# Scattering weighted expert rows by an accumulating DMA into one row per token

## The chip, the cores and the metric

The kernel runs on one core of a Trainium2 chip. The metric is the device time of one execution in microseconds (us). A profiled execution gives the trace; its own span and time stand in the table below.

## The reference, cut to what matters

```python
h = x + hybrid_mixer(rms_norm(x, norm_mix_g), ...)          # 512 tokens x 1024
xf = rms_norm(h, norm_ffn_g)
logits = xf @ w_router + b_router                            # 32 experts
top_vals, top_idx = lax.top_k(logits, 4); top_w = softmax(top_vals)
for each expert e, over the tokens that chose it:
    gu = x_e @ w_gate_up[e] + b_gate_up[e]                   # 1024 -> 2048
    gate = min(gu[:, :1024], 7); up = clip(gu[:, 1024:], -7, 7)
    y = ((up + 1) * gate * sigmoid(1.702 * gate)) @ w_down[e] + b_down[e]
    out[token] += top_w * y                                  # four experts for each token
return rms_norm(h + out, norm_final_g)
```

All numbers are float32. Each token has four choices, so there are 2048 (token, choice) pairs.

## The kernel before, in words

The first 670 us are the mixer, the router and the routing tables. The change bears on the second part, `mix_and_experts`, which each engine has once, and there on the experts.

**Items.** An item is one expert with up to 128 slots, one slot in each partition. Item i reads the weights of expert i; a second round of items exists only where an expert has more than 128 tokens. `last` is the number of the last item, here 31. `target` holds for each slot and item the number 4 x token + choice, or a number from 2048 up for an empty slot; `index` is `target` shifted right by two, which is the token.

**The loop.** Each engine runs a hardware loop over i = 0 to last - 1, and what is left of item `last` stands behind it.
- SyncE (SP) loads 12 chunks of 1 MB of weights per item into the six slots of `mraw`, each as soon as the chunk six before it is split.
- ScalarE rounds a chunk to float32r (`mhi`, L512), VectorE subtracts to get the rest (`mlo`, L516), TensorE takes three products of each pair: L2330, L2331 and L2333 for gate and up of item i + 1, L2351, L2352 and L2354 for down of item i.
- After the first chunk of down, TensorE turns the tokens `xg` that were gathered for item i + 2 (`turn_tokens`, L2308). It waits there for the gather.
- ScalarE copies the finished rows of item i from PSUM to `y_rows` (`y_copy`, L1280).
- GpSimd (POOL) does per pass: the product `hid` (L888); `scatter(i)`, a copy of a column of `target` to `now` (L891), a wait for `y_copy`, a tiny addition (`step`, L876), an indirect DMA of `y_rows` to memory (L895) and a wait until it has landed; then `gather(i + 3)`, a copy of a column of `index` (L879), `step`, and an indirect DMA that brings the tokens (L882).

The scatter writes row `target` of `y_d`, 2048 rows of 4 KB, one for each (token, choice) pair; empty slots are out of bounds and are left out. The rows of the last item are not scattered.

**The end.** When the last scatter has landed, POOL releases SP (`s_stored`). SP loads `norm_final_g` (L727) and then, for each of the four tiles of 128 tokens, the four rows of each of its tokens, 2 MB in two DMAs (L737). VectorE adds three of the four rows with their weights to the residual `h_rows` (`add_rows`, L1867). TensorE gathers in PSUM the down biases (`bias_product`, L2392), the rows of the last item through the 0/weight matrix `put_back` (`last_rows`, L2398) and the fourth row of each token through a diagonal of weights (`fourth_rows`, L2404). VectorE adds that (`add_products`, L1875), ScalarE sums squares (L1324), POOL makes the inverse root (L947, L949), VectorE scales (`finish`, L1880) and SP stores the tile (L741).

The order around the change is set by hand, by the program order of each engine and its semaphores:

```python
def scatter(i):
    nc.gpsimd.tensor_copy(now[:, 1:2], target[:, bass.ds(i, 1)]).then_inc(s_goal, 1)
    pool.wait_ge(s_goal, i + 1)
    pool.wait_ge(s_y, i + 2)
    step()
    nc.gpsimd.indirect_dma_start(y_d, ... now[:, 1:2] ..., y_rows[:], ...).then_inc(s_yst, 16)
    pool.wait_ge(s_yst, 16 * i + 16)
    pool.sem_inc(s_yfree, 1)
```

Names as the profile writes them: `zT` is `h_rows`, `glu` holds gate, up, sig and hid, `qkvT` holds `xn2`, `PB` is PSUM, `expert_rows_scratch` is `y_d`, `xn_scratch` holds the normed tokens.

## Time and profile before

| | us |
|---|---|
| median of 3 runs | 1855.16 (1854.9 to 1856.78) |
| the profiled execution's own time | 1855.72 |
| its span | 1854.0 |
| TensorE busy | 1805.2 (97%) |
| VectorE busy | 1473.2 (79%) |
| ScalarE busy | 1103.4 (60%) |
| GpSimd busy | 411.1 (22%) |

Granted TensorE clock over the span: 0.993 of full speed. The 16 DMA engines moved 507.80 MB, 274 GB/s on the mean. A busy TensorE is one whose matmuls follow each other; the time between the profiled execution and its span lies outside the span.

### The profile page before, as it was taken

How to read it: one execution, taken by the hardware profiler on the slowest of the kernel's cores; microseconds unless marked ns; L12 is line 12 of the kernel's file. 1: busy time of each engine (PE TensorE's matmuls, PEld its weight loads, DVE VectorE, ACT ScalarE, POOL GpSimd, SP SyncE). 2: the span in 40 equal slices, each digit the busy share in tenths (PEclk: the TensorE clock that was granted, in tenths of full speed). 3: DMA queues.
4: the chain of work that ended last, by engine and by line, in shares of the span. 5: the costliest groups of instructions: out<-in, count | busy, mean ns of one | idle time of the engine just before them, and what ended most of it. 6: DMA issues, size and time to landing. Idle time of an engine off the chain costs nothing.

```text
span 1854.0 us, 23922 instructions
## 1 busy us (share of the span) xinstructions
PE 1805.2 (97%) x8636; PEld 1502.9 (81%) x8636; DVE 1473.2 (79%) x1101; ACT 1103.4 (60%) x906; POOL 411.1 (22%) x332
## 2 busy tenths in 40 slices
PE   7999999999999999999999999999999999999995
PEld 6888888798888887888888888888888888888873
DVE  4236666765334689999999999999999999999996
ACT  4223563333332346777777777777777777777771
POOL 0000112420000018222222321322322222232231
PEclk9999999999999999999999999999999999999998
DMA  5323423005572538999999999999999999999976
GB/s 165 111 91 110 163 87 119 18 7 178 197 243 98 227 137 329 364 382 382 350 382 380 352 371 385 356 370 382 357 366 382 379 346 380 382 347 380 381 282 239
DMA packets 129774, 507.80 MB, mean 274 GB/s; under 512 B 26327, under 2 KB 26535, under 8 KB 95620
## 3 DMA queue, kind: packets, MB, share of 16 engines
q1 hardware_dynamic: 118276, 490.69, 69.4%
q0 software_dynamic: 9280, 16.27, 2.3%
q8 instruction: 29, 0.48, 0.1%
q10 hardware_dynamic: 2176, 0.26, 0.1%
q14 instruction: 13, 0.11, 0.0%
HBM read 492.46 MB, written 32.02 MB: 283 GB/s over the span
## 4 chain that ended last, share of the span: by engine, by line
PE 89%; DVE 6%; ACT 2%; DMA 1%; issue 1%; SPq 0%; POOL 0%; DVEq 0%; POOLq 0%; ACTq 0%
PE PB L2330 12%; PE PB L2331 12%; PE PB L2333 12%; PE PB L2249 11%; PE PB L2354 6%; PE PB L2351 6%; PE PB L2352 6%; PE PB L1934 4%; PE PB L1936 4%; PE PB L1935 4%; PE PB L2067 2%; PE PB L2320 2%; PE PB L2314 1%; PE PB L2308 1%; PE PB L2214 1%
## 5 line engine op out<-in xcount | busy, mean ns | idle before, releaser
L516 DVE TENSOR_TENSOR mlo<-mraw,mhi 128x2048 fp32r<-128x2048 f32 x384 | 906.5, 2395 | 48.2 <-ACT mhi L512 46.7
L512 ACT ACTIVATE mhi<-mraw 128x2048 fp32r<-128x2048 f32 x384 | 721.5, 1913 | 110.0 <-PE PB L2333 110.0
L2330 PE MATMUL PB<-mhi,xgT_hi 128*128 128x512 f32 x1024 | 403.1, 394 | 1.3 <-DVE mlo L516 1.3
L2331 PE MATMUL PB<-mlo,xgT_hi 128*128 128x512 f32 x1024 | 400.0, 391 | 0.0
L2333 PE MATMUL PB<-mhi,xgT_lo 128*128 128x512 f32 x1024 | 273.9, 389 | 0.0
L2330 PEld LDWEIGHTS PB<-mhi,xgT_hi 128*128 128x128 f32 x1024 | 192.7, 188 | 42.3 <-DVE mlo L516 1.4
L2333 PEld LDWEIGHTS PB<-mhi,xgT_lo 128*128 128x128 f32 x1024 | 192.3, 188 | 40.3
L2331 PEld LDWEIGHTS PB<-mlo,xgT_hi 128*128 128x128 f32 x1024 | 192.9, 188 | 39.5
L2351 PE MATMUL PB<-mhi,hT_hi 128*128 128x512 f32 x512 | 202.1, 395 | 1.1 <-DVE hT_lo L1831 1.1
L2352 PE MATMUL PB<-mlo,hT_hi 128*128 128x512 f32 x512 | 199.4, 389 | 0.0
L888 POOL TENSOR_TENSOR glu<-glu 128x1024 f32<-128x1024 f32 x32 | 78.8, 2462 | 522.5 <-DVE glu L1826 522.5
L2354 PE MATMUL PB<-mhi,hT_lo 128*128 128x512 f32 x512 | 158.0, 390 | 0.0
L1367 DVE TENSOR_TENSOR lo<-raw,hi 128x2048 fp32r<-128x2048 f32 x24 | 55.0, 2291 | 114.8 <-ACT hi L979 114.8
L1934 PE MATMUL PB<-xT_hi,hi 128*128 128x512 f32 x336 | 131.2, 390 | 0.7 <-ACT ab L1001 0.7
L1679 DVE TENSOR_TENSOR lo<-qkvT,hi 128x2048 fp32r<-128x2048 f32 x18 | 41.3, 2292 | 113.2 <-ACT hi L1192 113.2
L1935 PE MATMUL PB<-xT_lo,hi 128*128 128x512 f32 x336 | 130.7, 389 | 0.0
L1936 PE MATMUL PB<-xT_hi,lo 128*128 128x512 f32 x336 | 130.7, 389 | 0.0
L979 ACT ACTIVATE hi<-raw 128x2048 fp32r<-128x2048 f32 x26 | 49.8, 1914 | 127.8 <-PE PB L1936 105.0
L2351 PEld LDWEIGHTS PB<-mhi,hT_hi 128*128 128x128 f32 x512 | 96.2, 188 | 20.3 <-issue 1.5
L2354 PEld LDWEIGHTS PB<-mhi,hT_lo 128*128 128x128 f32 x512 | 96.1, 188 | 20.1
L2352 PEld LDWEIGHTS PB<-mlo,hT_hi 128*128 128x128 f32 x512 | 96.3, 188 | 18.9
L1192 ACT ACTIVATE hi<-qkvT 128x2048 fp32r<-128x2048 f32 x18 | 34.5, 1915 | 120.0 <-PE PB L2249 115.6
(359 smaller groups left out, 2572.9 us busy)
## 6 DMA issues: line engine op xcount, KB each, us to landing
mraw<-in_w_gate_up_dram SPq DMA_DIRECT2D x256, 1024.0 KB, 7.3
mraw<-in_w_down_dram SPq DMA_DIRECT2D x128, 1024.0 KB, 8.8
raw<-in_w_in_dram SPq DMA_DIRECT2D x28, 1024.0 KB, 5.1
qkvT<-in_w_in_dram SPq DMA_DIRECT2D x8, 1024.0 KB, 5.1
expert_rows_scratch<-zeros SPq DMA_DIRECT2D x4, 2048.0 KB, 11.4
mraw<-expert_rows_scratch SPq DMA_DIRECT2D x6, 1024.0 KB, 11.8
qkvT<-in_w_o_gdn_dram SPq DMA_DIRECT2D x4, 1024.0 KB, 6.4
qkvT<-in_w_o_sconv_dram SPq DMA_DIRECT2D x4, 1024.0 KB, 5.1
```

The costliest lines, as they stand in the source:

```text
L512: nc.scalar.activation(mhi[split_slot(m)][:], mraw[:, raw_slot(m), :], ACT.Copy).then_inc(e_h, 1)
L516: nc.vector.tensor_tensor(mlo[split_slot(m)][:], mraw[:, raw_slot(m), :], mhi[split_slot(m)][:].bitcast(F32), ALU.subtract).then_inc(e_l, 1)
L1934: pe.matmul(dst, w_hi, xT_hi[:, k, :], start=(k == 0), stop=False)
L1935: pe.matmul(dst, w_hi, xT_lo[:, k, :], start=False, stop=False)
L1936: mm = pe.matmul(dst, w_lo, xT_hi[:, k, :], start=False, stop=(k == KD - 1))
L2249: mm = pe.matmul(dst, lhsT, rhs, start=(k == 0 and n == 0), stop=(k == KD - 1 and n == 2))
L2330: pe.matmul(gate_up_bank[:, n, :], xgT_hi[:, k, :], w_hi[:, n, :], start=False, stop=False)
L2331: pe.matmul(gate_up_bank[:, n, :], xgT_hi[:, k, :], w_lo[:, n, :], start=False, stop=False)
L2333: mm = pe.matmul(gate_up_bank[:, n, :], xgT_lo[:, k, :], w_hi[:, n, :], start=False, stop=(k == KD - 1))
L2351: pe.matmul(y_bank[:, n, :], hT_hi[:, k, :], w_hi[:, kk, n, :], start=(k == 0), stop=False)
L2352: pe.matmul(y_bank[:, n, :], hT_hi[:, k, :], w_lo[:, kk, n, :], start=False, stop=False)
L2354: mm = pe.matmul(y_bank[:, n, :], hT_lo[:, k, :], w_hi[:, kk, n, :], start=False, stop=(k == KD - 1))
```

## The change

The scratch `y_d` of 2048 rows is replaced by `sum_d` of 512 + 128 rows, one row for each token and 128 spare ones. SP stores the residual `h_rows` to the first 512 (four DMAs of 512 KB, ahead of the loop) and clears the spare ones (one DMA of 512 KB; before, four DMAs of 2 MB cleared `y_d`). `scatter` adds in memory: its DMA has `compute_op=ALU.add`, takes the row from `index`, and an empty slot of partition p goes to spare row 512 + p (the table of targets is numbered so), so that all 128 rows are moved each time. The weights are applied before the scatter: `y_copy` multiplies each partition by `slot_weight`, a column that an indirect DMA (`slot_weights`) brings for the next item right behind each scatter, by a second copy into `now[:, 2:3]`. `put_back` is 0/1 and `by_weight` is gone. At the end SP loads one row per token (512 KB for each tile), straight into `h_rows`; the added rows (`add_rows`) and the fourth rows (`fourth_rows`) are gone.

```diff
-    y_d = nc.dram_tensor("expert_rows_scratch", (SEQ * TOPK, D), F32, kind="Internal").ap()
+    sum_d = nc.dram_tensor("token_sums_scratch", (SEQ + P, D), F32, kind="Internal").ap()
...
@@ SP
-                        if 2 <= g <= TT + 1:
+                        if g == 2:
                             sp.wait_ge(s_zeros, 1)
-                            sp.dma_start(y_d.rearrange("(t p r c) d -> t p (r c d)", t=TT, p=P, r=1)[g - 2].rearrange(
-                                "p (n c) -> p n c", c=GW), zeros[:].unsqueeze(1).to_broadcast([P, TOPK * D // GW, GW])
-                                         ).then_inc(s_ycl, 16)
+                            sp.dma_start(sum_d[SEQ:].rearrange("p (n c) -> p n c", c=GW),
+                                         zeros[:].unsqueeze(1).to_broadcast([P, D // GW, GW])).then_inc(s_ycl, 16)
...
                         sp.dma_start(xn2_d.rearrange("(t p) d -> p t d", p=P)[:, t, :], xn2[:, t, :]).then_inc(s_store, 16)
+                    for t in range(TT):
+                        sp.dma_start(sums_by_token[:, t, :], h_rows[:, t, :]).then_inc(s_hout, 16)
...
                     sp.wait_ge(s_stored, 1)
                     sp.dma_start(final_gain[:], norm_final_g.partition_broadcast(P)).then_inc(s_fg, 16)
                     for t in range(TT):
-                        if t == 0:
-                            sp.wait_ge(e_l, chunk_number(last, 0))
-                        elif t < TT - 1:
-                            sp.wait_ge(e_l, chunk_number(last, 2 * t - 1) + 1)
-                        else:
-                            sp.wait_ge(e_used, chunk_number(last, 3) + 1 + SPL)
-                        for half in range(2):
-                            w = slice(half * 2 * D, (half + 1) * 2 * D)
-                            sp.dma_start(rows_t[t].rearrange("p k d -> p (k d)")[:, w], y_by_token[t][:, w]
-                                         ).then_inc(s_pick[t][half], 16)
+                        sp.dma_start(h_rows[:, t, :], sums_by_token[:, t, :]).then_inc(s_back[t], 16)
@@ POOL
                     def scatter(i):
-                        nc.gpsimd.tensor_copy(now[:, 1:2], target[:, bass.ds(i, 1)]).then_inc(s_goal, 1)
+                        nc.gpsimd.tensor_copy(now[:, 1:2], index[:, bass.ds(i, 1)]).then_inc(s_goal, 1)
+                        pool.wait_ge(s_ws, 16 * i + 16)
+                        nc.gpsimd.tensor_copy(now[:, 2:3], target[:, bass.ds(i + 1, 1)]).then_inc(s_wrow, 1)
                         pool.wait_ge(s_goal, i + 1)
+                        pool.wait_ge(s_wrow, i + 2)
                         pool.wait_ge(s_y, i + 2)
                         step()
-                        nc.gpsimd.indirect_dma_start(y_d, bass.IndirectOffsetOnAxis(ap=now[:, 1:2], axis=0), y_rows[:], None,
-                                                     bounds_check=SEQ * TOPK - 1, oob_is_err=False).then_inc(s_yst, 16)
+                        nc.gpsimd.indirect_dma_start(sum_d, bass.IndirectOffsetOnAxis(ap=now[:, 1:2], axis=0), y_rows[:], None,
+                                                     compute_op=ALU.add, bounds_check=SEQ + P - 1, oob_is_err=True
+                                                     ).then_inc(s_yst, 16)
+                        slot_weights()
                         pool.wait_ge(s_yst, 16 * i + 16)
                         pool.sem_inc(s_yfree, 1)
+
+                    def slot_weights():
+                        nc.gpsimd.indirect_dma_start(slot_weight, None, w_d, bass.IndirectOffsetOnAxis(ap=now[:, 2:3], axis=0),
+                                                     bounds_check=SEQ * TOPK - 1, oob_is_err=False).then_inc(s_ws, 16)
...
-                    for t in range(TT):
-                        n = t * TOPK + TOPK - 1
-                        nc.gpsimd.tensor_scalar(by_weight[:, t, :], ident[:], weight[:, n:n + 1], None, ALU.mult).then_inc(s_byw, 1)
...
+                    pool.wait_ge(s_hout, 16 * TT)
@@ ACT
                         act.wait_ge(s_yfree, i + 1)
-                        nc.scalar.activation(y_rows[:].rearrange("p (b c) -> p b c", b=2), y_bank, ACT.Copy).then_inc(s_y, 1)
+                        act.wait_ge(s_ws, 16 * i + 16)
+                        nc.scalar.activation(y_rows[:].rearrange("p (b c) -> p b c", b=2), y_bank, ACT.Copy,
+                                             scale=slot_weight).then_inc(s_y, 1)
@@ DVE
                     def add_products(t):
+                        dve.wait_ge(s_back[t], 16)
                         dve.wait_ge(s_bo, 2 * t + 2)
-                        dve.wait_ge(s_added, added[0])
...
-                    add_rows(0, range(3))
-                    for t in range(TT):
-                        if t + 1 < TT:
-                            add_rows(t + 1, range(2))
+                    for t in range(2):
                         add_products(t)
-                        if t + 1 < TT:
-                            add_rows(t + 1, range(2, 3))
+                    dve.wait_ge(s_sum, 1)
+                    finish(0)
+                    for t in range(2, TT):
+                        add_products(t)
+                    dve.wait_ge(s_sum, TT)
+                    for t in range(1, TT):
                         finish(t)
@@ PE
                     last_rows(0)
-                    fourth_rows(0)
                     last_rows(1)
                     last_rows(2)
                     bias_product(3)
                     last_rows(3)
-                    for t in range(1, TT):
-                        fourth_rows(t)
```

One pass of POOL's loop before, from `hid` to the gather (ISA and REGISTER_ALU set registers):

```order
L888 TENSOR_TENSOR glu<-glu 128x1024
L891 ISA
L891 COPY now<-target 128x1
L876 TENSOR_TENSOR idle<-idle 128x1
L895 DMA expert_rows_scratch<-y_rows,now 2048x1024
L897 ISA
L879 ISA
L879 COPY now<-index 128x1
L876 TENSOR_TENSOR idle<-idle 128x1
L882 DMA xg<-xn_scratch,now 128x1024
```

and the same piece of POOL's loop with the change, where the lines of the changed file are counted:

```order
L877 TENSOR_TENSOR glu<-glu 128x1024
L880 ISA
L880 COPY now<-index 128x1
L881 ISA
L882 ISA
L882 COPY now<-target 128x1
L865 TENSOR_TENSOR idle<-idle 128x1
L887 DMA token_sums_scratch<-y_rows,now 640x1024
L895 DMA goal_f<-choice_weights_scratch,now 128x1
```

A second one-column copy stands between the first and the step, and a second indirect DMA behind the scatter; the copy of `index`, the step and the gather follow as before.

VectorE behind its loop, before (`zT` is `h_rows`; the first two rows of these are the last weight splits):

```order
L516 TENSOR_TENSOR mlo_88<-mraw,mhi_84 128x2048
L1867 SCALAR_TENSOR_TENSOR zT<-mraw,weight,zT 128x1024 x5
L1875 TENSOR_TENSOR zT<-PB,zT 128x1024
L1867 SCALAR_TENSOR_TENSOR zT<-mraw,weight,zT 128x1024
L1880 SCALAR_TENSOR_TENSOR zT<-zT,fstat,final_gain 128x1024
L1867 SCALAR_TENSOR_TENSOR zT<-mraw,weight,zT 128x1024 x2
L1875 TENSOR_TENSOR zT<-PB,zT 128x1024
```

and VectorE's whole end with the change:

```order
L515 TENSOR_TENSOR mlo_88<-mraw,mhi_84 128x2048
L1862 TENSOR_TENSOR zT<-PB,zT 128x1024 x2
L1867 SCALAR_TENSOR_TENSOR zT<-zT,fstat,final_gain 128x1024
L1862 TENSOR_TENSOR zT<-PB,zT 128x1024 x2
L1867 SCALAR_TENSOR_TENSOR zT<-zT,fstat,final_gain 128x1024 x3
```

All twelve additions of weighted rows are gone, and three of the four scalings stand at the very end.

## Rows read from the trace of the kernel before

**Rows 1.** One item's length: busy us of PE, PEld, DVE, ACT, POOL; clock; DMA share; GB/s.

```profile
1400.00:1435.40 35.40, 35.40 (x166) 29.42 (x165) 33.81 (x18) 26.54 (x18) 9.40 (x7) 1.00 0.95 371
```

**Rows 2.** Waits of PE from 745 us to the end: total, times, longest us.

```profile
PE PB L2404 <- DMA rows<-expert_rows_scratch: 3.0, 1, 3.0
```

**Rows 3.** Timeline of POOL through item 30: start us, us, what, idle before.

```profile
1762.85 2.39 POOL L888 TENSOR_TENSOR glu<-glu 128x1024 f32<-128x1024 f32 x1 [17.22 <-DVE glu L1826]
1765.20 2.24 POOL L891 COPY now<-target 128x1 uint32 x1
1768.59 1.06 POOL L876 TENSOR_TENSOR idle<-idle 128x1 f32<-128x1 f32 x1 [1.15 <-ACT y_rows L1280]
1769.81 1.07 POOL L895 DMA_INDIRECT expert_rows_scratch<-y_rows,now  x1 [0.15 <-issue]
1778.46 0.76 POOL L879 COPY now<-index 128x1 uint32 x1 [7.58 <-DMA expert_rows_scratch<-y_rows,now]
1779.31 0.19 POOL L876 TENSOR_TENSOR idle<-idle 128x1 f32<-128x1 f32 x1
1780.00 1.06 POOL L882 DMA_INDIRECT xg<-xn_scratch,now  x1 [0.50 <-issue]
```

**Rows 4.** Timeline of VectorE in the same stretch.

```profile
1763.81 5.79 DVE L516 TENSOR_TENSOR mlo<-mraw,mhi 128x2048 fp32r<-128x2048 f32 x2
1770.28 8.90 DVE L516 TENSOR_TENSOR mlo<-mraw,mhi 128x2048 fp32r<-128x2048 f32 x4 [0.68 <-ACT mhi L512]
1779.10 1.22 DVE L1831 TENSOR_TENSOR hT_lo<-PB,hT_hi 128x1024 fp32r<-128x1024 f32 x1
1780.30 6.83 DVE L516 TENSOR_TENSOR mlo<-mraw,mhi 128x2048 fp32r<-128x2048 f32 x3
```

**Rows 5.** Timeline of PE's weight loads: the turn of the gathered tokens.

```profile
1793.35 1.02 PEld L2308 LDWEIGHTS PB<-ident,xg 128*128 128x128 f32 x8
```

**Rows 6.** From issue to landing, the scatter L895, then the gather L882.

```profile
DMA to landing us min/median/max: 3.3/7.6/9.0
...
DMA to landing us min/median/max: 5.3/8.0/8.4
```

**Rows 7.** Columns as rows 1: the last scatter's data, then a stretch of the closing loads.

```profile
1806.80:1808.30 1.50, 1.50 (x7) 1.24 (x8) 1.23 (x1) 1.50 (x2) 0.00 (x0) 1.00 0.42 159
1823.00:1825.00 2.00, 2.00 (x6) 0.91 (x5) 1.90 (x2) 0.00 (x0) 0.00 (x0) 1.00 0.99 414
```

**Rows 8.** Columns as rows 1: the stretch behind the stores of `xn2`.

```profile
660.00:672.00 12.00, 12.00 (x109) 12.00 (x109) 8.28 (x28) 3.51 (x3) 0.95 (x1) 1.00 0.12 46
```

**Rows 9.** POOL ahead of its loop's first `hid`, then at the last scatter.

```profile
735.86 2.41 POOL L888 TENSOR_TENSOR glu<-glu 128x1024 f32<-128x1024 f32 x1 [3.72 <-DVE glu L1826]
...
1805.23 1.07 POOL L895 DMA_INDIRECT expert_rows_scratch<-y_rows,now  x1 [0.16 <-issue]
```

**Rows 10.** The end: the chain that ended last, one wait of it.

```profile
1811.54 10.80 DMA mraw<-expert_rows_scratch
```

**Rows 11.** The end: timeline of PE.

```profile
1818.59 1.96 PE L2398 MATMUL PB<-y_rows,put_back 128*128 128x512 f32 x4 [0.31 <-ACT y_rows L1319]
1820.38 1.88 PE L2404 MATMUL PB<-mraw,by_weight 128*128 128x512 f32 x4
1825.13 1.03 PE L2392 MATMUL PB<-b_out,mix_wT 96*128 96x512 f32 x2
```

**Rows 12.** The end: timeline of VectorE, and SP's load L727 with its landing.

```profile
1825.15 1.23 DVE L1875 TENSOR_TENSOR zT<-PB,zT 128x1024 f32<-128x1024 f32 x1
1828.59 1.28 DVE L1880 SCALAR_TENSOR_TENSOR zT<-zT,fstat,final_gain 128x1024 f32<-128x1024 f32 x1 [1.02 <-POOL fstat L949]
...
1848.29 1.28 DVE L1880 SCALAR_TENSOR_TENSOR zT<-zT,fstat,final_gain 128x1024 f32<-128x1024 f32 x1 [2.15 <-POOL fstat L949]
...
1810.14 0.34 SPq L727 DMA_DIRECT2D final_gain<-in_norm_final_g_dram  x1
...
DMA to landing us min/median/max: 4.4/4.4/4.4
```

More of the change, by code:

```diff
@@ L2398, in last_rows @@
                             pe.matmul(PM[:, BANK_OF_TILE[t] + n, :], put_back[:, t * P:(t + 1) * P],
[L2399 to L2405 removed]
+                                      y_rows[:, n * GW:(n + 1) * GW], start=False, stop=True).then_inc(s_bo, 1)
                     pe.wait_ge(s_mixc, 1)
```

59 lines of the change are left out of this document (20 added, 39 removed).

## The prediction

> **What bounds the kernel now.** First the busy time of one stretch as long as an item, from the middle of the loop [rows 1]: TensorE is busy in all of its 35.40 us, VectorE in 33.81, and the DMA engines are at 0.95 with 371 GB/s. Then the waits of TensorE from 745 us on [rows 2]: in 31 passes of the loop it waits for nobody worth a row, and its longest wait, 3.0 us, is at the end, for the last rows that come back. So the loop is worth something only if the change makes TensorE wait, and a gain has to come from the end. There the chain has one wait of 10.80 us for a load of expert rows [rows 10]; the eight loads of 1 MB keep the engines at 0.99 and 414 GB/s [rows 7], VectorE adds rows between them, and its last scaling starts at 1848.29 [rows 12], though TensorE had the last item's rows at 1818.59 [rows 11].
>
> A second thing is to be read before the sum: how POOL's small operations go. A one-element step takes 0.19 us at 1779.31, while VectorE reads PSUM (L1831, 1779.10 to 1780.31), and 1.06 us at 1768.59; the copy of one column takes 2.24 us at 1765.20 [rows 3]. The 1.06 ends at 1769.65, with the second of the two subtractions L516 that began at 1763.81 and ran 5.79 us in all, to 1769.60; the next begins 0.68 us later [rows 3, 4]. So a small POOL operation begun under L516 ends with it. The next four end by 1779.18, then come L1831 and three more, of 6.83 us: ends at about 1782.6, 1784.9 and 1787.1 [rows 4].
>
> **The loop, step by step**, with item 30's times. Before, the scatter is issued at 1769.81, seen landed and followed by the copy at 1778.46 (8.65 later), the gather is issued at 1780.00 [rows 3], lands 8.0 later (median) [rows 6], 1788.0, and TensorE takes the tokens at 1793.35 [rows 5]. Slack: 5.3 us.
> - *Second copy.* It starts at 1767.5, under L516, and ends at 1769.65. `y_copy` was awaited until 1768.59, so 1.1 us of it lies in a wait that was there. The step then starts at about 1769.9 and fits into the gap up to 1770.28 [rows 4]. Scatter at about 1770.25: +0.4 us. Bounds: 0, and +2.8 if the step misses the gap (it then ends with the next L516, at 1772.6). I take 0.4, since the gap of 0.68 us holds a 0.19 us step and two waits.
> - *The scatter itself.* Before there is no accumulating DMA, so its price has to be bounded. The last scatter, alone on the engines, is the cleanest row: its data moved in 1.50 us at a share of 0.42 and 159 GB/s, 0.24 MB or 58 rows [rows 7]. Now 128 rows go, and each is also read from memory. From below, nothing: less than half of the engines' time was used, so 70 more rows could fit beside the 58, with the reading hidden. From above, all in proportion: 128/58 rows times two passes is 4.4 times 1.50, 6.6 us, +5.1. I take +1.5, a doubling of the data phase: the unused share holds the new rows and the second read is paid. The row it is nearest to is the 1.50.
> - The Trainium skill, Collectives: The Full Stack, "The bandwidth ceiling: the fold count and why AG ≠ RS ≠ AR", says that an adding DMA is slower not by the add but by its two source reads, which halve its rate. By that too the data phase doubles; without it (the add free and the read hidden) the term would be 0 and the sum about 1 us lower. No run here shows it yet.
> - *`slot_weights`.* A DMA_INDIRECT costs POOL 1.07 us [rows 3], here inside the 7.58 us wait for the scatter: nothing. If that cover were gone it would be 1.1 us on the way to the gather. What queues behind it is only `gather(i + 3)`. `y_copy` needs its column one item later, some 25 us after it lands: nothing.
> - *`y_copy` with a per-row scale.* Nothing: up to 1.06 us more (1769.65 less 1768.59) hides behind the second copy.
> - *The gather behind it.* Copy of `index` ready at 1770.25 + 8.65 + 1.5 = 1780.4. That is just under the first of the three L516, so copy until 1782.65, then the step under the second until 1784.9, gather at about 1785.1, landed 8.0 later at 1793.1. TensorE asks at 1793.35. Slack 0.25 us; at the longest landing seen, 8.4 [rows 6], 0.15 us late. A scatter at its median of 7.6 instead of item 30's longer one has its copy ready near 1779.6, beside L1831, and the gather leaves 4 us earlier. So most items wait for nothing; I allow 1 us over the loop.
> - *The queue of weights.* Per item the scatter writes 0.26 MB more (64 rows more, since 2048 pairs over 32 items are 64 per item) and reads 0.52 MB: 0.79 MB in 35.4 us, 22 GB/s on 371. The closing loads show 414 [rows 7], so 393 fits: nothing.
>
> **The start.** Four stores of 0.5 MB more on SP, ahead of the loop: 2.1 MB are 5.1 us at 414 GB/s, and the engines are at 0.12 from 660 to 672 [rows 8], where they fall: nothing. If that cover were gone, the first weights would come 5 us later. The 7.9 MB of clears less lie under mixer products with TensorE busy: nothing. Without `by_weight` POOL is earlier at its first `hid`, where it waited 3.72 us for VectorE already [rows 9]: nothing.
>
> **The end.** The last scatter left at 1805.23 [rows 9]; now the second copy holds it until about 1805.65. It landed after 3.3 us [rows 6]; with +1.5 it lands at 1810.5. The copy of `index` then falls under the last L516 (to 1811.6), and SP is released some 0.7 us after it, at about 1812.3, where its load of the gain stood at 1810.14 [rows 12]: +2.2. Behind it come 2.1 MB instead of 8.4. The gain took 4.4 us alone [rows 12]; 0.5 MB are 1.3 us at 414 GB/s, so the tiles land at about 1818, 1819.3, 1820.6 and 1822. TensorE is later than that: a tile of `last_rows` takes 1.79 us (1818.59 to 1820.38) and the bias product about 0.9 of the 1.03 shown [rows 11], so tiles end at 1820.5, 1822.2, 1824.0 and 1826.4. The loads have left the path. Even with +5.1 for the scatter the first tile comes at 1821.6 and the last at 1825.6, which costs nothing at the last tile.
>
> VectorE: additions of 1.23 us [rows 12] at 1820.6 and 1822.3; the first scaling 2.2 us after the end of its addition, as before (1825.15 + 1.23 to 1828.59 [rows 12]), so 1824.1 to 1825.3; additions to 1826.5 and 1827.7; scalings of tiles 1 and 2 to 1829.0 and 1830.2. The last could start 2.25 us after 1827.7, at 1830.0, and starts at 1830.2. Before, it started at 1848.29: **-18.1 us**. The store behind it is the same, though three now follow each other closely.
>
> **Sum.** -18.1 + 1 + 0 = -17.1 on the profiled execution's own 1855.72 gives 1838.6; the median of the runs is 0.56 lower, so **1838 us**. Measurements of this kernel tell about 0.2% (3.7 us) from no change; below, faster and slower mean by more than that.
>
> **The rivals.**
> - *TensorE starves for tokens (slower).* If the copy of `index` is ready after 1782.6 instead of 1780.4, it ends with the second L516 (1784.9), the step with the third (1787.1), the gather leaves at 1787.3 and lands at 1795.3, 2.0 us after TensorE asks. Every later engine shifts with TensorE, so it is paid in each pass: 30 x 2.0 = 60 us, 1838 + 60 = 1898. It decides at a scatter 3.7 us dearer than item 30's before, or 1.2 us dearer with a missed gap. For it: the bound of +5.1, and slack already used up by two quanta. Against it: the engines' unused 0.58 in rows 7. Chance 0.20, of which a part falls on some items only.
> - *Small waits in the loop.* The slack of 0.25 us is overdrawn by 0.15 to 0.5 us in most items, by a longer landing under a fuller queue: 5 to 15 us, 1842 to 1853. Chance 0.13.
> - *The memory is full already.* The loop is at 0.95; if 393 GB/s is more than loads mixed with stores can reach (the 414 are loads alone) and the ceiling is, say, the 371 shown, then each item takes 0.79 MB / 371 GB/s = 2.1 us longer, 31 x 2.1 = 66, 1904. Against it: 0.05 of the engines' time is free, and 414 in the same kernel. Chance 0.03.
> - The Trainium skill, HBM Reference, "Specifications (TRN2)", gives 358 GB/s as a core's share of the memory, and that a core alone gets about 425. By the share the loop would be over the limit already and the change could only cost (0.79 MB are 2.2 us then, 1906); the rows with 371 and 414 agree with the figure for a core alone.
> - *The end does not pay.* The tiles come back late or TensorE's part is longer than worked out, so only half of the 18 is won: 1846 or so. Chance 0.04.
>
> **The numbers.** Forecast, 1834 to 1842: 0.60. Small waits 0.13, half an end 0.04, starving 0.20, full memory 0.03. Faster: 0.60 + 0.11 + 0.04 + a little of the partly starved = 0.76; same 0.04; slower 0.20. Below 1833 lies next to nothing (the end would have to gain over 22). Up to 1866 lie the forecast, the small waits and the cases where fewer than half the items starve: 0.80.
>
> **What would show it.** Right: the item's length stays 35.4 us with TensorE busy throughout; POOL's second copy of about 2.2 us; scatter to landing about 9.5 us in the loop and 4.8 at the last; the gather issued 1 to 5 us later in the item; no additions L1867 at the end, tiles landed before TensorE's products, the last scaling some 18 us earlier. Wrong: a wait of TensorE at the turn of `xg` for the gather, 31 times; an item longer than 35.4; scatter to landing above 12 us; ScalarE waiting for weights.

## The result, and the profile after

The changed kernel takes **1872.93 us** (median of 4 runs, 1871.05 to 1875.78); the kernel before, beside it on the same chip, 1855.97 us (4 runs, 1854.90 to 1857.27). The ratio is 1.0092, 95% interval 1.0077 to 1.0107: slower by 17 us, where 17 us less were forecast. 1872.93 lies 7 us above the upper end of the range. One slow execution of the kernel before, of 3723 us, beside the first experiments is left out of all ratios.

The first and the last `hid` of POOL cut the span into three parts. In the profiled executions (spans 1854.0 and 1871.4, clock 0.995 after the change) they give:

| part | before, us | after, us | difference | forecast |
|---|---|---|---|---|
| start to first `hid` | 704.3 | 705.7 | +1.4 | 0 |
| first to last `hid` (31 items) | 1094.0 | 1127.1 | +33.1 | +1 |
| last `hid` to the end | 55.7 | 38.5 | -17.2 | -18.1 |

So the end came as worked out and the loop ate it twice over. The waits of PE from 745 us on, where [rows 2] had one wait of 3.0 us at the end (total, times, longest us):

```profile
PE PB L2296 <- DMA xg<-xn_scratch,now: 27.7, 15, 2.1
```

The wait for the last rows is gone; fifteen waits for gathered tokens (L2296 turns `xg`) are new. By the weight loads of the same line they are 34.0 us, about the 33.1 of the table. The loop alternates between a pass that ends in such a wait and one that doesn't. POOL's timeline through one of each (start us, us, what, idle before), to be laid beside [rows 3]:

```profile
1101.91 2.40 POOL L877 TENSOR_TENSOR glu<-glu 128x1024 f32<-128x1024 f32 x1 [17.10 <-DVE glu L1824]
1104.26 2.24 POOL L880 COPY now<-index 128x1 uint32 x1
1106.44 2.26 POOL L882 COPY now<-target 128x1 uint32 x1
1108.84 0.20 POOL L865 TENSOR_TENSOR idle<-idle 128x1 f32<-128x1 f32 x1
1109.60 3.70 POOL L887 DMA_INDIRECT token_sums_scratch<-y_rows,now  x1 [0.56 <-issue]
...
1121.03 0.75 POOL L868 COPY now<-index 128x1 uint32 x1 [6.08 <-DMA token_sums_scratch<-y_rows,now]
1121.87 2.12 POOL L865 TENSOR_TENSOR idle<-idle 128x1 f32<-128x1 f32 x1
1124.14 2.95 POOL L871 DMA_INDIRECT xg<-xn_scratch,now  x1
1137.32 2.42 POOL L877 TENSOR_TENSOR glu<-glu 128x1024 f32<-128x1024 f32 x1 [10.23 <-DVE glu L1824]
...
1145.27 0.20 POOL L865 TENSOR_TENSOR idle<-idle 128x1 f32<-128x1 f32 x1 [1.15 <-ACT y_rows L1275]
1146.04 1.63 POOL L887 DMA_INDIRECT token_sums_scratch<-y_rows,now  x1 [0.57 <-issue]
...
1156.04 1.05 POOL L871 DMA_INDIRECT xg<-xn_scratch,now  x1
```

VectorE in the same two passes ([rows 4] before), and the weight load that waits for the tokens ([rows 5]):

```profile
1109.51 8.90 DVE L515 TENSOR_TENSOR mlo<-mraw,mhi 128x2048 fp32r<-128x2048 f32 x4 [0.85 <-ACT mhi L511]
1118.32 1.22 DVE L1829 TENSOR_TENSOR hT_lo<-PB,hT_hi 128x1024 fp32r<-128x1024 f32 x1
1119.46 6.74 DVE L515 TENSOR_TENSOR mlo<-mraw,mhi 128x2048 fp32r<-128x2048 f32 x3
...
1146.94 8.90 DVE L515 TENSOR_TENSOR mlo<-mraw,mhi 128x2048 fp32r<-128x2048 f32 x4 [2.86 <-ACT mhi L511]
1155.76 1.22 DVE L1829 TENSOR_TENSOR hT_lo<-PB,hT_hi 128x1024 fp32r<-128x1024 f32 x1
```

```profile
1134.56 0.86 PEld L2296 LDWEIGHTS PB<-ident,xg 128*128 128x128 f32 x8 [2.19 <-DMA xg<-xn_scratch,now]
```

Three readings. The step at 1108.84 did fit the gap of VectorE, which ends at 1109.51. Its DMA did not: it begins at 1109.60, 0.56 us behind the step's end, 0.09 us after the subtraction L515, and takes 3.70 us instead of the 1.63 of the next pass, where TensorE's stall has widened the gap to 2.86 us. And the gather's DMA at 1124.14, begun under the three subtractions from 1119.46, takes 2.95 us, against 1.05 at 1156.04 beside L1829, which reads PSUM. The two lines over all items ([rows 6] before): both have a short and a long form.

```profile
L887 POOL DMA_INDIRECT token_sums_scratch<-y_rows,now x31: 1619/1636/3731, 745.0 to 1840.5; - x31
...
DMA to landing us min/median/max: 5.9/8.5/13.6
...
L871 POOL DMA_INDIRECT xg<-xn_scratch,now x32: 1024/1042/2957, 702.9 to 1847.7; - x32
...
DMA to landing us min/median/max: 5.1/8.3/10.5
```

The two passes by windows (columns as [rows 1]): the first is as long as before, since its wait falls into its last 5 us and moves only the next `hid`; the second is 2.02 us longer.

```profile
1101.91:1137.32 35.41, 33.64 (x156) 27.68 (x156) 33.71 (x18) 24.70 (x17) 17.86 (x9) 1.00 0.95 358
1137.32:1174.75 37.43, 37.43 (x174) 31.10 (x173) 33.24 (x18) 28.48 (x19) 14.90 (x10) 1.00 1.00 380
```

Counted from an item's `hid`, the chain to its tokens reads so:

| us after `hid` | before, item 30 | forecast | after, pass at 1101.91 |
|---|---|---|---|
| scatter's DMA begins | 6.96 | 7.40 | 7.69 |
| scatter landed, copy of `index` begins | 15.61 | 17.55 | 19.12 |
| gather's DMA begins | 17.15 | 22.25 | 22.23 |
| tokens landed | 25.15 | 30.25 | 32.6 |
| TensorE asks for them | 30.50 | 30.50 | 30.46 |

(32.6 is 1134.56 less 1101.91, and the ask lies 2.19 before it.) In this pass the gather left within 0.02 us of the forecast, and its landing is what missed. So it is in 11 of the 15 passes that end in a wait. In the other four the scatter is seen only 21.0 to 21.6 us after `hid`, so that the copy and the step each begin one subtraction later; the gather then leaves at 24.49, in its short form, and lands 8.4 to 8.5 us later. One of the four, where TensorE waits 2.49 us:

```profile
1614.15 2.40 POOL L877 TENSOR_TENSOR glu<-glu 128x1024 f32<-128x1024 f32 x1 [17.68 <-DVE glu L1824]
...
1635.70 0.53 POOL L868 COPY now<-index 128x1 uint32 x1 [8.49 <-DMA token_sums_scratch<-y_rows,now]
...
1638.64 1.03 POOL L871 DMA_INDIRECT xg<-xn_scratch,now  x1
```

The end, in order: TensorE at the last item's rows; SP's loads of the sums; VectorE's last two scalings (the operation of [rows 12]); and, out of the chain that ended last, POOL's operations for these two tiles.

```profile
1853.52 5.39 PE L2386 MATMUL PB<-y_rows,put_back 128*128 128x512 f32 x12 [0.48 <-ACT y_rows L1316]
```

```profile
1848.04 2.02 SPq L727 DMA_DIRECT2D zT<-token_sums_scratch  x4
```

```profile
1864.71 1.28 DVE L1867 SCALAR_TENSOR_TENSOR zT<-zT,fstat,final_gain 128x1024 f32<-128x1024 f32 x1 [0.76 <-POOL fstat L943]
1866.74 1.28 DVE L1867 SCALAR_TENSOR_TENSOR zT<-zT,fstat,final_gain 128x1024 f32<-128x1024 f32 x1 [0.74 <-POOL fstat L943]
```

```profile
1862.77 1.27 POOL fstat L941
1864.11 0.57 POOL fstat L943
1864.76 1.31 POOL fstat L941
```

### The profile page after: what moved, and what is told of

The parts are those of the page before. It is cut to its first block, busy times and chain, and to the rows that moved or that the text cites. A ratio compares the mean times of both kernels' runs of the same rounds, so it can differ in the third digit from the quotient of the medians.

```text
span 1871.4 us, 24012 instructions
## 1 busy us (share of the span) xinstructions
PE 1804.8 (96%) x8620; PEld 1501.5 (80%) x8620; DVE 1446.5 (77%) x1089; ACT 1105.6 (59%) x906; POOL 598.6 (32%) x390
## 3 DMA queue, kind: packets, MB, share of 16 engines
HBM read 486.18 MB, written 26.26 MB: 274 GB/s over the span
## 4 chain that ended last, share of the span: by engine, by line
PE 56%; DMA 18%; issue 9%; DVE 6%; POOL 5%; ACT 4%; POOLq 0%; SPq 0%; DVEq 0%; ACTq 0%
PE PB L2237 10%; DMA token_sums_scratch<-y_rows,now 9%; DMA xg<-xn_scratch,now 8%; PE PB L2318 6%; PE PB L2319 6%; PE PB L2321 6%; PE PB L1922 4%; PE PB L1923 4%; PE PB L1924 4%; PE PB L2339 3%; PE PB L2340 3%; PE PB L2342 3%; PE PB L2055 2%; POOL now L880 2%; POOL now L882 2%
## 5 line engine op out<-in xcount | busy, mean ns | idle before, releaser
L515 DVE TENSOR_TENSOR mlo<-mraw,mhi 128x2048 fp32r<-128x2048 f32 x384 | 896.5, 2371 | 92.2 <-ACT mhi L511 92.2
```

Source lines behind the costliest of these rows:

```text
L515: nc.vector.tensor_tensor(mlo[split_slot(m)][:], mraw[:, raw_slot(m), :], mhi[split_slot(m)][:].bitcast(F32), ALU.subtract).then_inc(e_l, 1)
```

## The experiments

The theory behind them: the copies, steps and DMA instructions of POOL meet VectorE's subtractions in the slack that the gather had, and the new work (a second copy ahead of the scatter's DMA, the adding, 128 rows instead of 64, a gather of weights) has used it up. The rivals: the adding scatter is simply too long; the number of rows; the DMA of the slot weights; memory. Where no number of runs is given below, the time is that of a single run. The kernel before, timed beside them, lay between 1854.7 and 1859.4 us, so a few us in a single run say little; its profile says more.

### 1. The gather ahead of `hid`

```
                     with pool.Fori(0, last) as i:
+                        pool.wait_ge(s_tx, i + 2)
+                        gather(i + 3)
                         pool.wait_ge(s_th, i + 1)
                         hidden(i + 1)
                         scatter(i)
-                        pool.wait_ge(s_tx, i + 2)
-                        gather(i + 3)
```

> The changed kernel with one edit: POOL does the gather of tokens for item i + 3 ahead of the product and the scatter, as soon as TensorE has turned the tokens before, some 10 us earlier in the item. Theory A (TensorE's 15 waits of 2 us come only from the gather that stands behind the scatter): no wait of TensorE at the turn of xg, items of 35.4 us, 1838 us (18 us of the end kept). Theory B (the adding scatter fills the DMA engines, so that some load is late whatever the order): TensorE or ScalarE waits elsewhere, 1855 to 1873 us.

Measured: 1859.32 us (11 runs), ratio to the kernel before 1.0015 (1.0006 to 1.0024). No wait for tokens is left, so the tokens were the loop's loss. But the items are 36.0 us long. What TensorE waits for now is VectorE:

```profile
PE PB L2318 <- DVE mlo L515: 9.7, 29, 0.4
```

Its weight loads for the same products wait 22.4 us in all, and the loop is 19.4 us longer than that of the kernel before. POOL's `hid` leaves about a microsecond later, behind the gather's DMA, and lies with its whole length beside the first subtraction.

### 2. The same order in the kernel before

The same edit in the kernel before tells whether that belongs to the order.

> The kernel before with the gather ahead of hid alone. Theory A2 (it is the place of the gather that makes the items 36.0 us, through VectorE, and nothing of the adding scatter): 36.0 us items here too, 1855 + 18 = 1873 us. Theory B (the adding scatter makes them long): 35.4 us, 1855 us.

Measured: 1875.61 us, items of 36.0 us, and again 29 waits:

```profile
PE PB L2330 <- DVE mlo L516: 9.8, 29, 0.3
```

It belongs to the order. The adding scatter isn't needed for it.

### 3. The scatter without its addition

```
-                                                     compute_op=ALU.add, bounds_check=SEQ + P - 1, oob_is_err=True
+                                                     bounds_check=SEQ + P - 1, oob_is_err=True
```

The rows are written in place of the sum and not added: that part of the computation is left out.

> The changed kernel, the scatter writes instead of adding (the sums are left out; the same 128 rows move). Theory A (the add makes POOL's DMA instruction longer, 1.63 us and 0.56 us of issue instead of 1.07 and 0.15, so that it starts just under VectorE's next subtraction and takes 3.70): the instruction is back at 1.07, lands in about 8 us every time, no waits, 1838 to 1842 us. Theory C (the second copy and the second indirect DMA cost the time, not the add): 1865 to 1873 us as before.

Measured: 1865.56 us, 11 waits for tokens, 19.2 us in all. So some 7 us of the 17 go with the addition, and more than half of the loss stays. Theory A was wrong: the plain DMA begins at 7.69 us after `hid` too, under the same subtraction, and is short only in the passes that follow a wait and at the last item. The scatter's line shows what it costs by itself:

```profile
L887 POOL DMA_INDIRECT token_sums_scratch<-y_rows,now x31: 1074/3159/3177, 743.3 to 1827.6; - x31
...
DMA to landing us min/median/max: 3.5/9.5/11.0
```

The shortest landing is 3.5 us, against 5.9 with the addition and 3.3 in [rows 6], where some 60 rows went: the addition is 2.4 us, the further rows 0.2. These are single landings with little beside them; in the loop, in passes that don't follow a wait, the median from the DMA's begin until the copy is 10.05 us here and 11.43 with the addition. As an instruction on POOL the short form is 1.07 instead of 1.63 us, and the long form 3.16 instead of 3.70: the 2 us of the long form have nothing to do with adding.

### 4. Only the rows in use

The 64 empty slots of an item are dropped by the bound instead of being added to spare rows.

```
-                                                     compute_op=ALU.add, bounds_check=SEQ + P - 1, oob_is_err=True
+                                                     compute_op=ALU.add, bounds_check=SEQ - 1, oob_is_err=False
```

> The changed kernel, empty slots are out of bounds and are left out, 64 rows per item on the mean instead of 128. Theory A: the DMA instruction still starts 0.1 us under the subtraction and takes 3.70 us in every other item; the landing comes about 1 us earlier, which the copy's and the step's quanta swallow: 1865 to 1873 us. Theory E (the 64 spare rows with their reads are what makes the scatter late): waits gone or halved, 1840 to 1857 us.

Measured: 1880.93 us, 15 waits, 28.8 us. Half the rows bring nothing. Of the 8 us above the changed kernel, 2.0 lie ahead of the first `hid` and 5.8 in the loop, where four passes take some 39.3 us; no run tells why. The line:

```profile
L887 POOL DMA_INDIRECT token_sums_scratch<-y_rows,now x31: 1614/1631/3744, 747.0 to 1848.3; - x31
...
DMA to landing us min/median/max: 6.0/6.9/11.4
```

The shortest landing is 6.0 with the rows in use and 5.9 with 128. In a long pass the scatter begins at 1114.15 and the copy behind it at 1125.80, 11.65 us, as with all rows (11.43). So the time that the addition adds to a landing doesn't grow with the rows. The DMA engines' own time does. The last scatter, nearly alone on the engines, by windows (columns as [rows 1]; share and GB/s are the last two): plain with some 58 rows, plain with 128 (experiment 3), adding some 58 (this run), adding 128 (the changed kernel).

```profile
1806.00:1809.00 3.00, 2.36 (x10) 1.99 (x11) 2.43 (x2) 2.84 (x2) 0.51 (x2) 1.00 0.21 79
1829.00:1831.00 2.00, 2.00 (x7) 1.57 (x6) 1.92 (x1) 1.85 (x2) 1.04 (x1) 0.55 0.67 262
1850.00:1854.50 4.50, 4.50 (x21) 3.73 (x20) 4.11 (x2) 1.39 (x1) 2.62 (x1) 1.00 0.36 53
1842.00:1846.50 4.50, 4.50 (x21) 3.72 (x20) 4.33 (x2) 1.61 (x1) 2.76 (x2) 1.00 0.74 117
```

Length times share is the time of all 16 engines together: 0.63 and 1.34 us plain, 1.62 and 3.33 us adding. Per row an addition takes 2.5 times as much, with either number of rows, though both adding scatters take about 4 us from first to last byte. For the reason that I took from the Trainium skill (Collectives: The Full Stack, "The bandwidth ceiling: the fold count and why AG ≠ RS ≠ AR": the add needs two source reads, and the rate is half) this means: the engines' time agrees in kind, at 2.5 and not 2; the landing doesn't follow it, since it is no longer with 128 rows than with 58. What sets the 4 us stays open.

### 5. No slot weights in the loop

```
-                        pool.wait_ge(s_ws, 16 * i + 16)
-                        nc.gpsimd.tensor_copy(now[:, 2:3], target[:, bass.ds(i + 1, 1)]).then_inc(s_wrow, 1)
...
-                        slot_weights()
```

Every item is scaled by the weights of item 0; the gathers and copies for the others are left out (and ScalarE waits for the first weights alone).

> The changed kernel without the second copy and without the gather of slot weights in the loop (every item is scaled with the weights of item 0). Theory A: the step then ends with the subtraction, as before the change, the adding scatter starts 0.4 to 0.5 us earlier, ahead of VectorE's next subtraction, and takes 1.63 us: no waits or nearly none, 1838 to 1842 us. Theory D (the adding scatter alone is too long for the slack): waits stay, 1860 us or more.

Measured: 1848.47 us, 4 waits:

```profile
PE PB L2292 <- DMA xg<-xn_scratch,now: 7.3, 4, 2.0
```

The adding scatter of 128 rows is in it untouched, and most of the loss is gone: the scatter's DMA now begins ahead of the subtraction in every pass, and its line reads 1626/1630/1679 ns. From its begin until the copy of `index` the median is 9.57 us, against 7.87 in the kernel before: adding and the further rows are +1.7 us in the loop. That alone is too long in 4 passes only. Copy or gather is the next question.

### 6. The gather of weights moved behind the gather of tokens

```
                         scatter(i)
                         pool.wait_ge(s_tx, i + 2)
                         gather(i + 3)
+                        slot_weights()
```

(and out of `scatter`, where it stood.)

> The changed kernel with one DMA moved: the gather of the next item's slot weights is issued behind the gather of tokens instead of between the scatter and POOL's wait for its landing. The second copy stays where it is. Leaving out the weights, their copy and their gather together gave 1848.5 and 4 long passes instead of 15. Theory one, the copy is what cost (it pushes the step and the scatter's DMA under VectorE's subtraction): moving the DMA changes next to nothing, 1868 to 1878 us, some 15 waits of about 1.9 us for the tokens. Theory two, the gather's descriptors beside the scatter's made the scatter land later: 4 or so long passes, 1848 to 1856. A part of both: in between, with the number of waits telling the share.

Measured: 1876.83 us, 15 waits, 28.1 us. The place of that DMA decides nothing, which leaves the copy. In two passes of this run, as in four of the changed kernel, the copy of `index` begins only under the second subtraction and the gather goes off at 24.50 us after `hid` instead of 22.24.

### 7. The second copy alone, in the kernel before

```
                         nc.gpsimd.tensor_copy(now[:, 1:2], target[:, bass.ds(i, 1)]).then_inc(s_goal, 1)
+                        nc.gpsimd.tensor_copy(now[:, 2:3], target[:, bass.ds(i, 1)]).then_inc(s_extra, 1)
                         pool.wait_ge(s_goal, i + 1)
+                        pool.wait_ge(s_extra, i + 1)
```

> The kernel before with one more copy of one column between scatter's copy and its step, used by nothing. Theory A2: this alone moves the scatter's DMA under VectorE's next subtraction; it takes 3 us instead of 1.07, the landing comes 3 to 4 us later, and TensorE waits 2 us for its tokens in many passes: 1868 to 1885 us. Theory F (a copy of 0.2 us costs nothing, only the add and the additional DMA do): 1855 us.

Measured: 1859.0 us, one wait of 1.8 us for tokens. I expected 9 us more at least, and was wrong about the sum though not about the longer DMA. One of its latest passes:

```profile
1126.54 2.40 POOL L889 TENSOR_TENSOR glu<-glu 128x1024 f32<-128x1024 f32 x1 [14.72 <-DVE glu L1829]
...
1134.22 2.99 POOL L898 DMA_INDIRECT expert_rows_scratch<-y_rows,now  x1 [0.55 <-issue]
1143.85 0.18 POOL L880 COPY now<-index 128x1 uint32 x1 [6.64 <-DMA expert_rows_scratch<-y_rows,now]
...
1146.48 2.93 POOL L883 DMA_INDIRECT xg<-xn_scratch,now  x1 [0.15 <-issue]
```

Both DMAs are in their long form, by the copy alone: 2.99 and 2.93 us, where [rows 3] has 1.07 and 1.06. But the scatter is seen 17.31 us after `hid` here, just ahead of the three subtractions, and the gather leaves at 19.94. The median landing of the gather is 10.4, so the tokens are in at 30.3, and TensorE asks at 30.5. Most passes have more room: the median of the seen scatter is 17.05 (14.84 in the kernel before, so the copy costs 2.2 us), and in 24 of the 28 passes that neither wait nor follow a wait the gather has left by 18.13. The one pass that waits is the one whose scatter is seen at 17.61. With the same copy and 128 rows, not added, plus the weights' DMA (experiment 3), the median is 17.74. A pass of it that waits: the scatter is seen at 17.93 after `hid` (1113.64 less 1095.71), the copy of `index` falls under the subtractions, the gather leaves at 22.23, and TensorE waits 2.18 us. With the addition it is 19.12, under the same subtraction, and the gather leaves at the same 22.23.

So the loss is a threshold. In the nine traces where the gather follows the scatter there are 206 passes that don't follow a wait: in the 141 without a wait the scatter is seen by 17.51 us after `hid`, in the 65 with one (of 2.1 us or more, but for one of 0.4) at 17.56 or later. The three subtractions begin at 17.55 (1119.46 less 1101.91 in the changed kernel). What carried the scatter over it: the copy ahead of it, with the long form of its DMA, which that causes (+2.2 us); and the addition with the further rows (+1.7). The kernel before has its median 2.7 us below the threshold, so either alone stays under it in most passes and both together in none.

### 8. The second copy behind the scatter's DMA

```
                     def scatter(i):
                         nc.gpsimd.tensor_copy(now[:, 1:2], index[:, bass.ds(i, 1)]).then_inc(s_goal, 1)
-                        pool.wait_ge(s_ws, 16 * i + 16)
-                        nc.gpsimd.tensor_copy(now[:, 2:3], target[:, bass.ds(i + 1, 1)]).then_inc(s_wrow, 1)
                         pool.wait_ge(s_goal, i + 1)
-                        pool.wait_ge(s_wrow, i + 2)
...
                                                      ).then_inc(s_yst, 16)
+                        pool.wait_ge(s_ws, 16 * i + 16)
+                        nc.gpsimd.tensor_copy(now[:, 2:3], target[:, bass.ds(i + 1, 1)]).then_inc(s_wrow, 1)
+                        pool.wait_ge(s_wrow, i + 2)
+                        step(2)
                         slot_weights()
```

> The changed kernel with the second copy (and a step of its own) behind the scatter's DMA, ahead of the gather of slot weights. Theory A2 (POOL's DMA needs some 0.7 us from the start of the step; if the step is not itself blocked until the subtraction ends, the DMA falls under the next one, takes 2 us more and its packets start 4 us later): the step is blocked again by the awaited y_copy's place, the DMA starts in the gap and takes 1.63 us, waits in a few items only, as without slot weights: 1845 to 1852 us. Theory C (the gather of slot weights itself delays the landing): 1862 us or more.

One run gave 1841.40 us, with one wait for tokens. The same kernel again, with more runs:

> The version that only moves the second copy and a step for it behind the scatter's DMA, timed in rounds beside the others (one look gave 1841.4, with one wait of 1.8 us for the tokens in the loop). Theory: the one step of the program that cost the loop is the second copy in front of the DMA, so this gives 1839 to 1845 us, at most 4 waits for tokens of about 1.9 us each. Rival: the one look was lucky, and timed runs scatter over 1841 to 1860 as items fall into the long pass or not.

Measured: 1842.09 us (5 runs, 1839.80 to 1845.79), ratio to the kernel before 0.9927 (0.9913 to 0.9941), with two waits for tokens of 3.8 us in all. One pass: the step ends with the subtraction that it waited out, and the DMA follows 0.16 us behind it, in the gap.

```profile
1126.81 2.40 POOL L877 TENSOR_TENSOR glu<-glu 128x1024 f32<-128x1024 f32 x1 [16.98 <-DVE glu L1825]
...
1132.71 0.90 POOL L865 TENSOR_TENSOR idle<-idle 128x1 f32<-128x1 f32 x1 [1.32 <-ACT y_rows L1276]
1133.77 1.63 POOL L884 DMA_INDIRECT token_sums_scratch<-y_rows,now  x1 [0.17 <-issue]
...
1143.85 0.18 POOL L868 COPY now<-index 128x1 uint32 x1 [1.77 <-DMA token_sums_scratch<-y_rows,now]
```

The scatter is seen at 17.04 after `hid` here (median 16.67), under the threshold, with the addition, 128 rows and the weights' DMA all there; the two passes that wait are those where it is seen at 17.56 and 17.75. One copy's place turns +17 us into -13.

### 9. The gather between `hid` and the scatter

```
                         hidden(i + 1)
-                        scatter(i)
                         pool.wait_ge(s_tx, i + 2)
                         gather(i + 3)
+                        scatter(i)
```

> The changed kernel with the gather of tokens between the product hid and the scatter. Theory A2 (the loss is the gather behind the scatter; with the gather ahead of hid it was moved to VectorE, whose first subtraction of an item grew from 3.6 to 4.8 us because hid came 1 us later and fell on it; items of 36.0 us): here hid stands where it was, the gather leaves some 10 us before it did, nobody waits, items of 35.4 us, 1838 us. Theory B2 (POOL's operations under VectorE's subtractions slow VectorE wherever they stand): items near 36.0 us again, 1857 to 1860.

Measured: 1840.97 us (4 runs, 1839.06 to 1841.29), ratio to the kernel before 0.9911 (0.9894 to 0.9927). No wait for tokens at all, and every item takes 35.41 us. One item:

```profile
1127.43 2.41 POOL L877 TENSOR_TENSOR glu<-glu 128x1024 f32<-128x1024 f32 x1 [14.64 <-DVE glu L1824]
...
1134.39 1.05 POOL L871 DMA_INDIRECT xg<-xn_scratch,now  x1 [0.16 <-issue]
...
1141.94 3.50 POOL L887 DMA_INDIRECT token_sums_scratch<-y_rows,now  x1 [0.15 <-issue]
```

```profile
1127.43:1162.84 35.41, 35.41 (x165) 29.43 (x165) 33.70 (x18) 26.54 (x18) 19.94 (x9) 1.00 1.00 380
```

The scatter is in its long form here and leaves 7.5 us later than in experiment 8, at a median of 11.9 us to landing, and it costs nothing: nobody on the way to the tokens waits for it. The whole load, 380 GB/s with the DMA share at 1.00, fits with TensorE busy throughout, so the memory is no bound of this loop.

### 10. The same order in the kernel before, and both cures together

> The kernel before, with the order of the fastest version so far: hid, then the gather of tokens, then the scatter. It tells how much of that version's lead over the kernel before is the order alone. My theory: none. In the kernel before TensorE waits for nobody in the loop, so an earlier gather has nothing to shorten: 1855 to 1859 us, items of 35.4 us, ratio within 0.2% of 1. The lead is then the end alone. Rival: the order gives the loop something by itself (VectorE's additions or the landings come out better), then 1845 or less with items under 35.4 us. Second rival: it costs, as the gather in front of hid did (+0.6 us an item): 1875.

Measured: 1859.34 us (10 runs), ratio 1.0016 (1.0007 to 1.0025), first to last `hid` 1094.0 us as in the kernel before. The order gives the old loop nothing. The median is 4 us above that of the kernel before beside it; in the profiled executions 2.6 us of that lie ahead of the first `hid` and 2.6 behind the last. So what experiment 9 gains over the kernel before is the end of the change: 39.2 us behind the last `hid` instead of 55.7.

> Both cures together: hid, then the gather of tokens, then the scatter's DMA, and the second copy behind that. Each alone took the loop to items of 35.4 us, TensorE's own length. Theory: TensorE bounds the loop in each, so they do not add: 1839 to 1842 us, items 35.4 us, no wait for tokens. Rival: the earlier scatter also frees the rows y earlier or relieves VectorE, and the time falls below 1837. Second rival: the copy behind the scatter now holds up hid of the next item, a wait of TensorE for the products of hid, 1845 or more.

Measured: 1840.65 us (5 runs, 1838.19 to 1842.61), ratio 0.9917 (0.9904 to 0.9931), no wait for tokens. Its interval covers the values of the two single cures: they don't add, since TensorE bounds the loop in each. Of the versions that leave nothing out these three beat both kernels; by their intervals they can't be told apart.

## Why the prediction was wrong

**The steps that failed** are two, by one oversight. I had read from the trace that a small POOL operation begun under L516 ends with it, and applied that to copies and steps and not to the DMA instructions. In its loop the kernel before has none there; but ahead of it, once, it has: the gather of weights for item 0 begins under the third of four subtractions and takes 2.93 us, which ends about 1 us after that subtraction. The trace of the kernel before held the length that the forecast lacked.

```profile
713.46 2.93 POOL L924 DMA_INDIRECT goal_f<-choice_weights_scratch,goal  x1 [0.16 <-issue]
```

```profile
708.76 8.88 DVE L516 TENSOR_TENSOR mlo<-mraw,mhi 128x2048 fp32r<-128x2048 f32 x4
```

- *Second copy: "Scatter at about 1770.25: +0.4 us."* It is +2.2: the median of the seen scatter goes from 14.84 us after `hid` to 17.05 with the copy alone (experiment 7). The step fitted the gap, as worked out. The DMA behind it missed it by 0.09 us, since it begins 0.56 us after the step's end. [rows 3] had both values: 0.15 behind a step of 1.06 us and 0.50 behind one of 0.19. I counted the step and took the DMA for issued with it. The bound of +2.8 was tied to the step missing the gap; it should have been tied to the DMA.
- *The gather behind it: "gather at about 1785.1, landed 8.0 later at 1793.1".* The 8.0 was the median of DMAs that POOL began beside a read of PSUM [rows 3, 4, 6]; the forecast itself put this one under a subtraction, and there it takes 2.95 us as an instruction and lands 10.4 us after its start. That made a slack of 0.25 us a wait of 2.19.

Neither does it alone. Without the copy's 2.2 us two passes wait instead of fifteen (experiment 8). And with a landing of 8.0 a gather that left at 22.24 would have been in at 30.24, ahead of the ask; that is an estimate, no run has it.

That the gather left at 22.23 where 22.25 was forecast is luck. The chain was reckoned from item 30, whose scatter is seen 0.8 us later than the median of the kernel before; it put the copy of `index` at 17.55 us after `hid`, on the threshold itself; and the 1.6 us by which that fell short were swallowed by one subtraction. For a scatter at its median the forecast said that the gather leaves 4 us earlier and that most items wait for nothing; in fact no pass that doesn't follow a wait has its scatter seen before 19.05.

**The adding scatter, +1.5.** About right: +1.7 in the loop with the further rows (experiment 5). Its shortest landing is 2.6 us longer (5.9 against 3.3), of them 2.4 the addition and 0.2 the rows; within the bounds of 0 to 5.1. In four passes it takes some 2 us more than in the others, which moves the gather by another subtraction; why, no run tells.

**`slot_weights`, `y_copy`: nothing.** Right for the DMA (experiment 6) and for ScalarE, which has no wait for weights in the profile. Its copy was priced in the term above.

**The queue of weights: nothing.** Right: experiment 9 does all of it in items of 35.41 us. The rival of the full memory fell with that. The profile counts 377 GB/s from 745 to 1800 us there, against 369 before, and not 22 more: it shows the same 486.18 MB read with the addition and without (experiment 3), so the reads of an addition aren't in its count. Here the Trainium skill (HBM Reference, "Specifications (TRN2)") gives 358 GB/s as a core's share and some 425 for a core alone; 380 in a whole item, without a wait of TensorE, agrees with the second.

**The rival of the starving TensorE** came true in its effect, at half its size, and only in part by its own way. Its way was a copy of `index` ready after 1782.6, with the gather at 24.45 us after `hid`; so it goes in four of the fifteen passes (24.49). In the other eleven the gather leaves as in the forecast and lands late. The price of 2.0 us a wait is near the measured 2.1 to 2.6 in both, in the eleven by luck. It is paid in 15 passes instead of 30, since each wait widens VectorE's gap for the next pass from 0.85 to 2.86 us, the scatter's DMA falls into it, takes its short form and the gather leaves 3.5 us earlier in the item (18.72 after `hid`). That self-healing wasn't in the price of 60 us, and a rival with it would have come to 1838 + 30 = 1868, which is 5 us off. Giving it 0.20, and cutting the range at 1866, came from the slack of 0.25 us that I trusted over 31 items although it hung on one landing.

**The start: nothing.** +1.4 us. The first `hid` lies between 703.3 and 707.8 us over all versions, and between 703.4 and 706.9 in those of the kernel before alone, so it is no more than their scatter.

**The end, -18.1.** -17.2 from the last `hid`, of them -16.1 up to the last scaling and -1.1 behind it. TensorE's part and the loads were as worked out: the loads begin at 1848.04, and TensorE's tiles run through from 1853.52 without a wait for them. What was missed is POOL's part: the last two scalings are 2.03 us apart (1864.71 to 1866.74), not 1.2, since the root for each tile is two POOL operations of 1.3 and 0.57 us in a row. (The last tile of the forecast adds up to 1826.8, not 1826.4; that moves its last scaling by 0.1 us.)

## What to carry to other kernels

Where an engine's small instructions end with another engine's large ones, slack is counted in those quanta: price a chain by writing down under which instruction each link begins, DMA instructions included, and treat a forecast slack smaller than one quantum as none. Reckon from the spread of all passes and not from one: here the median said "no wait" and the one item "just in time", and neither showed how near the threshold was. An index or offset that a later transfer needs is prepared behind the transfer that somebody waits for, not ahead of it. And order a queue by who waits: the tokens of the next item were needed in 30 us, the scatter's landing by nobody before the next item's rows.

## What the runs showed of the hardware that I had not expected

- POOL's indirect DMA instruction (gather of tokens or plain scatter) takes 1.02 to 1.13 us begun in a gap of VectorE's subtractions or beside one of its reads of PSUM, and 2.6 to 3.2 begun under a subtraction of two SBUF tiles; the adding scatter 1.62 to 1.68 and 3.49 to 3.74. The long one goes by quanta too: it ends about 0.9 us (the adding scatter 1.5 to 1.7) after the subtraction under which it began. The gathers of experiment 7 that begin 17.7 to 18.1 us after `hid` all end near 20.7, where the first of the three subtractions ends at 19.7.
- With the long form the landing is later too, by about the instruction's own 2 us: in the changed kernel gathers in the long form land 10.3 to 10.5 us after their start, the four in the short form 8.4 to 8.5; the adding scatter is seen after 11.43 us in its long form and after 9.57 in its short one (medians, the changed kernel and experiment 5).
- The Trainium skill (SBUF — State Buffer, "Who interferes with whom") says that a VectorE instruction with two SBUF inputs contends with a GpSimd instruction that reads SBUF; the copies, the steps and these DMAs agree. The same section infers that descriptor generation isn't held up by such a subtraction; the 2 us show that an indirect DMA, whose operands include its column of offsets (`now`), is. Which part of the instruction is held, no run shows.
- Behind a step that was itself held up the DMA begins 0.15 us later, behind a free one 0.50 to 0.57. A stalled step is in this respect the cheaper one.
- An accumulating scatter costs some 2.4 us of its shortest landing whether it adds 58 or 128 rows of 4 KB, and 0.56 us more on POOL; per row it holds the DMA engines 2.5 times as long as a plain one (experiment 4).
- POOL's `hid` begun 1 us later, wholly beside a subtraction of VectorE, made each item 0.6 us longer through VectorE (experiments 1 and 2).

Open: what sets the 4 us that the adding scatter's bytes take, why it takes 2 us more in four passes of the changed kernel, and what part of the 0.7 us between the medians of experiments 3 and 7 (17.74 and 17.05) is the rows and what the weights' DMA.
